# Input tiles whose high and low halves lie behind each other, at a fixed distance from the weight tiles

## The chip, the cores and the metric

The kernel runs on one core of a Trainium2 chip. The metric is the time of one execution in device microseconds; lower is better.

## The reference, cut to what matters

One inference step of a decoder trunk, for 256 prompt tokens and 8 x 4 sample tokens, 288 rows in all, in float32 with a model width of 2048:

```python
x = x + 0.5 * swiglu(rms_norm(x, norm_ffn1), ffn1_w_gu, ffn1_w_down)     # 2048 -> 2 x 5632 -> 2048
z = rms_norm(x, norm_mix) @ w_in                                         # 2048 -> 13600
o_ret, o_rwkv = retention(z, state_ret), rwkv7(z, state_rwkv, state_shift)
merged = sigmoid(zgr) * (o_ret @ w_ret_o) + sigmoid(zgw) * (o_rwkv @ w_rwkv_o)
x = x + merged @ w_out
x = x + 0.5 * swiglu(rms_norm(x, norm_ffn2), ffn2_w_gu, ffn2_w_down)
y = rms_norm(x, norm_final)                                              # and the new states
```

## The kernel before, in words

Everything is kept transposed: the model width lies on the 128 partitions, in tiles of `[128, T]` with T = 288 columns, one per token. An input of a matrix product is a row of such tiles, k = 0 to 15 (21 for g, 7 for ow), each 288 x 4 = 1152 bytes in each partition.

The large products are made more exact by splitting. Each float32 operand is written as a high part, rounded to TensorE's faster float32 form (F32R), and a low part, the rest. Weights arrive from HBM by the SP queue in blocks of `[128, 2048]`, 16 tiles of 128 x 128, into the two slots of `raw`. ACT copies a block into `w_hi` (line 1068, halves at a time in line 1077), DVE subtracts into `w_lo` (line 1495, or 1489), and a wait on `lo_made` lets TensorE start on the block; `used` gives the slots back. A down projection's block has 1408 columns. Inputs are split in the same way: `h_hi`, `h_lo` (normalized x, for the gate and up projections and most of the mixing projections), `g_hi`, `g_lo` (the hidden layer, lines 1133 and 1563, two tiles at a time), `xg_hi`, `xg_lo` (the normalized x of the first mixing projections), `or`, `ow` (the outputs of retention and RWKV) and `m` (merged, lines 1454 and 2130).

For each weight tile `products` in the tensor block issues three matmuls, and each brings its own weight load:

```python
pe.matmul(out, wh, xh, start=start, stop=False)      # line 528
pe.matmul(out, wh, xl, start=False, stop=False)      # line 529
return pe.matmul(out, wl, xh, start=False, stop=stop)  # line 530
```

`pair` (lines 533 to 557) walks over two output tiles and all k: for k, for m in 0 and 1, `products` with column tile 2k + m of the weights and input tile k, into PSUM bank m of the pair. `piece` (from line 631) does a sixteenth of a block in the same way; in the mixing stage `weave` sets such pieces between the steps of retention and RWKV, by the shares in GAPS, so that TensorE has work while DVE, ACT and GpSimd go through the serial steps. TensorE's order is that of the program; weight loads are shown as an engine of their own, PEld, and run beside the matmul before.

SBUF is laid out by hand. `sb` gives out addresses from a running place in steps of 32 bytes, or puts a tile at a given address. `raw` and `w_hi` take 16384 bytes each. Before the change `w_lo`, `h_hi` and `h_lo` follow directly, and all lie at the same place modulo 256; `g_hi`, `g_lo`, `m_hi`, `m_lo`, `ow_hi` and `ow_lo` start 64 bytes behind it modulo 256, `xg_hi` and `xg_lo` 192 bytes, `or_hi` 32 and `or_lo` 64 bytes. The high halves of all k stand together, and then the low halves of all k.

Of the kernel before, what the change touches and what calls it, by code (L numbers as in the profile page):

```python
# [23 lines left out]
F32, F32R = mybir.dt.float32, mybir.dt.float32r  # L24
ALU, ACT = mybir.AluOpType, mybir.ActivationFunctionType

P = 128
D = 2048
KT = D // P
FF = 5632  # L30
HALF = FF // 2
HT = HALF // P
SEQ, SB, ST = 256, 8, 4
NS = SB * ST
T = SEQ + NS
# [3 lines left out]
PAIRS = RW // P  # L39
# [21 lines left out]
GATE_PAIRS = 2 * D // (2 * P)  # L61
GATE_BLOCKS = 2 * GATE_PAIRS
PARTS = 16
LOW_AT = (3, 10)
FIRST_MIX = (2, 5, 8, 11, 14)

# [35 lines left out]
def parts(blocks):  # L102

    total, seen, out = sum(w for _, w in GAPS), 0, {}
    for name, w in GAPS:
        first = round(PARTS * blocks * seen / total)
        seen += w
        out[name] = range(first, round(PARTS * blocks * seen / total))
    return out
# [7 lines left out]
def build(nc, d):  # L117
    with ExitStack() as ctx:
        place = [-(-nc.sbuf_base // 32) * 32]

        def sb(name, shape, dt=F32, at=None):

            size = int(np.prod(shape[1:])) * 4
            offset = place[0] if at is None else at
            if at is None:
                place[0] += -(-size // 32) * 32
            return nc.alloc_sbuf_tensor_at("sb_" + name, list(shape), dt, offset=offset)
# [5 lines left out]


        raw = sb("raw", [P, 2, BLK])
        w_hi = sb("w_hi", [P, 2, BLK], F32R)
        w_lo = sb("w_lo", [P, 2, BLK], F32R)
        h_hi = sb("h_hi", [P, KT, T], F32R)
        h_lo = sb("h_lo", [P, KT, T], F32R)
        mean_w = sb("mean_w", [P, P])  # L140
        head_w = sb("head_w", [P, P], F32R)
        ident = sb("ident", [P, P])
        gains = sb("gains", [P, 4, KT])
        eps_c = sb("eps_c", [P, 2])
        first_root = sb("first_root", [P, 1])
        arena = place[0]


        x = sb("x", [P, KT, T])
        g_hi = sb("g_hi", [P, HT, T], F32R)  # L150
        g_lo = sb("g_lo", [P, HT, T], F32R)
        gate = sb("gate", [P, 2, T])
        prod = sb("prod", [P, 2, T])
        sq = sb("sq", [P, 2, T])
        sum_sq = sb("sum_sq", [P, 2, T])
        scale = sb("scale", [P, T])
        xg_at = place[0]
        xg_hi = sb("xg_hi", [P, KT, T], F32R)
        xg_lo = sb("xg_lo", [P, KT, T], F32R)
        first_sq = sb("first_sq", [P, KT, T], at=xg_at)  # L160
        ffn_end = place[0]

# [4 lines left out]
        mix = place[0]  # L167
# [14 lines left out]
        tri = sb("tri", [P, 2, CH])  # L182
        tri_s = sb("tri_s", [P, 2, CH])
        eye = sb("eye", [P, CH])
        own = sb("own", [P, SB])
        run_m = sb("run_m", [P, T])
        last = sb("last", [P, 6, 1 + SB])
        rot = sb("rot", [P, 2, T])
# [91 lines left out]
        gate_z = sb("gate_z", [P, 2, 2, T], at=zs_at)  # L280

        place[0] = mix
        or_hi = sb("or_hi", [P, RH * VT, T], F32R, at=qk_at)
        assert qk_at + 4 * RH * VT * T <= trig_end
        or_lo = sb("or_lo", [P, RH * VT, T], F32R, at=arena)
        part = sb("part", [P, KT, T], at=mix + 8 * KT * T)
        ow_at = mix + 12 * KT * T + 24 * T
        ow_hi = sb("ow_hi", [P, PAIRS, T], F32R, at=ow_at)
        ow_lo = sb("ow_lo", [P, PAIRS, T], F32R, at=ow_at + 4 * PAIRS * T)
        m_hi = sb("m_hi", [P, KT, T], F32R, at=mix)  # L290
        m_lo = sb("m_lo", [P, KT, T], F32R, at=mix + 4 * KT * T)
        gate_m = sb("gate_m", [P, 2, 2, T], at=mix + 12 * KT * T)
        prod_m = sb("prod_m", [P, 2, T], at=mix + 12 * KT * T + 16 * T)
        assert max(ffn_end, pair_end, ow_at + 8 * PAIRS * T) <= nc.sbuf_usable_end


# [129 lines left out]
        class Weave:  # L426
# [6 lines left out]
            def __call__(self, gap):  # L433
                assert self.left.pop(0) == gap, gap
                for n in self.share[gap]:
                    self.piece(*divmod(n, PARTS))

# [88 lines left out]
        def _(pe):  # L526
# [91 lines left out]
            def projections(i):  # L618
                for n in range(MIX_BLOCKS):
                    for q in range(PARTS):  # L620
                        if n == 2 and q == 0:
# [1808 lines left out]
```

## Time and profile before

| | us |
|---|---|
| median of 3 runs | 2896.09 (2895.13 to 2897.52) |
| span of the profiled execution | 2893.1 |
| TensorE busy in it | 2869.7 |
| weight loads (PEld) | 2797.0 |
| DVE | 1564.2 |
| ACT | 1116.4 |
| GpSimd | 107.0 |

The times are those of whole executions. The profiled execution is one of its own; its total is told by its span alone, from its first instruction to its last, and lies 3.0 us under the median of the runs. The span goes through the first feed-forward (to about 845 us), the mixing stage (to 1780 us, with the gates' projections at its end), the output projections (to 2035 us) and the second feed-forward. A group's line gives line, engine, operation, tiles written and read, shapes and count, then the busy time, the mean length of one record in ns, and the idle time before it. Records of matmuls overlap, and their ends are modelled: a start is measured, a length is not.

### The profile page before, as it was taken

Reading aid. Unit: us, or ns where it says so; the run is one execution under the profiler, and the core shown is the slowest. Engines: PE = TensorE matmul, PEld = TensorE weight load, DVE = VectorE, ACT = ScalarE, POOL = GpSimd, SP = SyncE. Lnnn points to the kernel's source line nnn. Section 1 sums busy time; section 2 is a strip of 40 time slices with the busy share of each in tenths; the row PEclk is TensorE's granted clock in tenths of the full one; section 3 lists DMA queues with packets and bytes.
Section 4 is the critical chain, followed back from the end, with each engine's and each line's share of the span. In section 5 each row is a group of like instructions: output and inputs, shape, how many; then the busy total and the mean of one; then the engine's idle time right before and its main releaser. Section 6 shows DMA issues by size and latency. Waiting matters only on the chain.

```text
span 2893.1 us, 57249 instructions
## 1 busy us (share of the span) xinstructions
PE 2869.7 (99%) x24662; PEld 2797.0 (97%) x24662; DVE 1564.2 (54%) x1679; ACT 1116.4 (39%) x1121; POOL 107.0 (4%) x144
## 2 busy tenths in 40 slices
PE   9999999999999999999999999999999999999998
PEld 9999999999999999898999999999999999999998
DVE  6444444444557576775765555465544444444454
ACT  5333333333344353544534644233333333333333
POOL 0000000000000002011020010000000000000000
PEclk9999999999999999999999999999999999999999
DMA  5444444444456553635436544555444444444444
GB/s 208 161 162 163 160 169 175 159 164 153 169 185 221 184 193 110 247 133 199 160 130 237 180 153 164 186 201 190 163 162 162 163 160 169 175 160 165 153 168 142
DMA packets 85460, 495.80 MB, mean 171 GB/s; under 512 B 10320, under 2 KB 10496, under 8 KB 44096
## 3 DMA queue, kind: packets, MB, share of 16 engines
q1 hardware_dynamic: 71424, 444.14, 43.5%
q0 software_dynamic: 9280, 32.72, 3.1%
q10 hardware_dynamic: 4608, 16.78, 1.5%
q8 instruction: 116, 1.90, 0.3%
q14 instruction: 32, 0.26, 0.0%
HBM read 462.80 MB, written 30.80 MB: 171 GB/s over the span
## 4 chain that ended last, share of the span: by engine, by line
PE 94%; DVE 3%; ACT 2%; DMA 1%; issue 0%; SPq 0%; ACTq 0%; DVEq 0%
PE psum L528 29%; PE psum L529 29%; PE psum L530 29%; PE psum L876 1%; DVE sb_w_lo L1489 1%; PE psum L692 1%; PE psum L728 0%; DMA sb_raw<-in_gu 0%; DMA sb_raw<-in_w_wo 0%; PE psum L649 0%; ACT sb_w_hi L1077 0%; DVE sb_w_lo L1495 0%; ACT sb_w_hi L1068 0%; PE psum L889 0%; PE psum L886 0%
## 5 line engine op out<-in xcount | busy, mean ns | idle before, releaser
L528 PE MATMUL psum<-sb_h_hi,sb_w_hi 128*128 128x288 f32 x4384 | 1315.3, 300 | 3.6 <-DVE sb_w_lo L1489 1.4
L530 PE MATMUL psum<-sb_h_hi,sb_w_lo 128*128 128x288 f32 x4384 | 1295.1, 295 | 0.0
L529 PE MATMUL psum<-sb_h_lo,sb_w_hi 128*128 128x288 f32 x4384 | 1294.0, 295 | 0.0
L1495 DVE TENSOR_TENSOR sb_w_lo<-sb_raw,sb_w_hi 128x2048 fp32r<-128x2048 f32 (+1 forms) x348 | 712.4, 2047 | 723.8 <-ACT sb_w_hi L1068 723.2
L1068 ACT ACTIVATE sb_w_hi<-sb_raw 128x2048 fp32r<-128x2048 f32 (+1 forms) x349 | 600.3, 1720 | 1226.9 <-PE psum L530 1191.9
L528 PEld LDWEIGHTS psum<-sb_h_hi,sb_w_hi 128*128 128x128 f32 x4384 | 824.6, 188 | 27.8 <-issue 18.9
L529 PEld LDWEIGHTS psum<-sb_h_lo,sb_w_hi 128*128 128x128 f32 x4384 | 824.6, 188 | 1.3 <-issue 1.0
L530 PEld LDWEIGHTS psum<-sb_h_hi,sb_w_lo 128*128 128x128 f32 x4384 | 824.9, 188 | 0.0
L529 PE MATMUL psum<-sb_g_lo,sb_w_hi 128*128 128x288 f32 x1408 | 416.8, 296 | 0.0
L530 PE MATMUL psum<-sb_g_hi,sb_w_lo 128*128 128x288 f32 x1408 | 414.9, 295 | 0.0
L528 PE MATMUL psum<-sb_g_hi,sb_w_hi 128*128 128x288 f32 x1408 | 413.8, 294 | 0.0
L1489 DVE TENSOR_TENSOR sb_w_lo<-sb_raw,sb_w_hi 128x1024 fp32r<-128x1024 f32 x204 | 254.0, 1264 | 119.9 <-ACT sb_w_hi L1077 116.0
L528 PEld LDWEIGHTS psum<-sb_g_hi,sb_w_hi 128*128 128x128 f32 x1408 | 264.8, 188 | 0.0
L530 PEld LDWEIGHTS psum<-sb_g_hi,sb_w_lo 128*128 128x128 f32 x1408 | 264.6, 188 | 0.0
L529 PEld LDWEIGHTS psum<-sb_g_lo,sb_w_hi 128*128 128x128 f32 x1408 | 264.6, 188 | 0.0
L1077 ACT ACTIVATE sb_w_hi<-sb_raw 128x1024 fp32r<-128x1024 f32 x198 | 198.7, 1053 | 140.1 <-PE psum L530 109.1
L1545 DVE TENSOR_TENSOR sb_prod<-psum,sb_scale 128x576 f32<-128x576 f32 x44 | 33.3, 757 | 93.8 <-PE psum L530 93.8
L1556 DVE TENSOR_TENSOR sb_gate<-psum,sb_scale 128x576 f32<-128x576 f32 x44 | 33.3, 757 | 84.1 <-PE psum L530 84.0
L528 PE MATMUL psum<-sb_or_hi,sb_w_hi 128*128 128x288 f32 x256 | 76.0, 297 | 0.0
L529 PE MATMUL psum<-sb_m_lo,sb_w_hi 128*128 128x288 f32 x256 | 75.8, 296 | 0.0
L530 PE MATMUL psum<-sb_m_hi,sb_w_lo 128*128 128x288 f32 x256 | 75.5, 295 | 0.0
L530 PE MATMUL psum<-sb_or_hi,sb_w_lo 128*128 128x288 f32 x256 | 75.4, 295 | 0.0
(380 smaller groups left out, 2391.4 us busy)
## 6 DMA issues: line engine op xcount, KB each, us to landing
sb_raw<-in_gu SPq DMA_DIRECT2D x175, 1024.0 KB, 4.8
sb_raw<-in_down SPq DMA_DIRECT2D x128, 704.0 KB, 4.0
sb_raw<-in_w_mix SPq DMA_DIRECT2D x72, 1024.0 KB, 4.9
sb_raw<-in_w_gates SPq DMA_DIRECT2D x32, 1024.0 KB, 5.4
sb_s_ret<-in_s_ret POOLq DMA_DIRECT2D x32, 512.0 KB, 8.1
out_ret_s<-sb_s_ret ACTq DMA_DIRECT2D x32, 512.0 KB, 5.3
sb_raw<-in_w_ro SPq DMA_DIRECT2D x16, 1024.0 KB, 4.8
sb_raw<-in_w_out SPq DMA_DIRECT2D x16, 1024.0 KB, 4.8
```

What stands on the lines that cost most here:

```text
L528: pe.matmul(out, wh, xh, start=start, stop=False)
L529: pe.matmul(out, wh, xl, start=False, stop=False)
L530: return pe.matmul(out, wl, xh, start=False, stop=stop)
L692: mm = pe.matmul(psum[j * NS:(j + 1) * NS, bank, :], q_own[:, e, SLOTS * half + j, :], s_ret[:, 2 * e + j // 2, j % 2, :], start=(e == 0 a ...
L876: mm = pe.matmul(psum[w, 5, (t - 1) * CH:t * CH], lm[v, t, :], xm[v, t, :], start=True, stop=True)
L1068: act.activation(w_hi[:, slot, 0:cols], raw[:, slot, 0:cols], ACT.Copy).then_inc(hi_made, 2)
L1077: act.activation(w_hi[:, slot, c], raw[:, slot, c], ACT.Copy).then_inc(hi_made, 1)
L1489: dve.tensor_tensor(w_lo[:, slot, c], raw[:, slot, c], w_hi[:, slot, c].bitcast(F32), ALU.subtract).then_inc(lo_made, 1)
L1495: dve.tensor_tensor(w_lo[:, slot, 0:cols], raw[:, slot, 0:cols], w_hi[:, slot, 0:cols].bitcast(F32), ALU.subtract).then_inc(lo_made, 2)
L1545: dve.tensor_tensor(prod[:, :, :], psum[:, s:s + 2, 0:T], twice(scale), ALU.mult).then_inc(up_scaled, 1)
L1556: dve.tensor_tensor(gate[:, :, :], psum[:, s:s + 2, 0:T], twice(scale), ALU.mult).then_inc(gate_scaled, 1)
```

## The change

It adds two constants and two helpers to the layout. `align(apart)` moves the running place on to a fixed distance behind `w_hi` modulo 256. `halves_of` makes one tile in which the high half of tile k is followed at once by its low half: a pair takes 2304 bytes, nine times 256. It starts 144 bytes behind `w_hi` modulo 256 (128 by `align`, and 16 by four elements that stay unused in front). `w_lo` is moved to 128 bytes behind `w_hi` modulo 256. h, g, xg, ow and m are made by `halves_of`; `or_hi` and `or_lo` stay as they are, apart from the shift of what lies before them. `own`, `eps_c` and `first_root` are moved into the space that aligning leaves. No instruction is added or taken away, and no wait, count or loop is changed; what the instructions read and write is the same data at other addresses.

```diff
@@ -61,6 +61,7 @@
 GATE_PAIRS = 2 * D // (2 * P)
 GATE_BLOCKS = 2 * GATE_PAIRS
 PARTS = 16
+LINES, APART = 256, 144
 LOW_AT = (3, 10)
 FIRST_MIX = (2, 5, 8, 11, 14)
 
@@ -133,30 +134,45 @@
 
 
         raw = sb("raw", [P, 2, BLK])
+        weights_at = place[0]
         w_hi = sb("w_hi", [P, 2, BLK], F32R)
+        eps_c = sb("eps_c", [P, 3])
+        first_root = eps_c[:, 2:3]
+        own = sb("own", [P, SB])
+
+        def align(apart):
+
+            place[0] += (weights_at + apart // 32 * 32 - place[0]) % LINES
+
+        def halves_of(name, tiles, at=None):
+
+            if at is None:
+                align(APART)
+            ahead = APART % 32 // 4
+            both = sb(name, [P, ahead + 2 * tiles * T], F32R, at=at)
+            both = both[:, ahead:].rearrange("p (k two t) -> p k two t", two=2, t=T)
+            return both[:, :, 0, :], both[:, :, 1, :]
+
+        align(4 * T % LINES)
         w_lo = sb("w_lo", [P, 2, BLK], F32R)
-        h_hi = sb("h_hi", [P, KT, T], F32R)
-        h_lo = sb("h_lo", [P, KT, T], F32R)
+        h_hi, h_lo = halves_of("h", KT)
         mean_w = sb("mean_w", [P, P])
         head_w = sb("head_w", [P, P], F32R)
         ident = sb("ident", [P, P])
         gains = sb("gains", [P, 4, KT])
-        eps_c = sb("eps_c", [P, 2])
-        first_root = sb("first_root", [P, 1])
         arena = place[0]
 
 
         x = sb("x", [P, KT, T])
-        g_hi = sb("g_hi", [P, HT, T], F32R)
-        g_lo = sb("g_lo", [P, HT, T], F32R)
+        g_hi, g_lo = halves_of("g", HT)
         gate = sb("gate", [P, 2, T])
         prod = sb("prod", [P, 2, T])
         sq = sb("sq", [P, 2, T])
         sum_sq = sb("sum_sq", [P, 2, T])
         scale = sb("scale", [P, T])
+        align(APART)
         xg_at = place[0]
-        xg_hi = sb("xg_hi", [P, KT, T], F32R)
-        xg_lo = sb("xg_lo", [P, KT, T], F32R)
+        xg_hi, xg_lo = halves_of("xg", KT)
         first_sq = sb("first_sq", [P, KT, T], at=xg_at)
         ffn_end = place[0]
 
@@ -182,7 +198,6 @@
         tri = sb("tri", [P, 2, CH])
         tri_s = sb("tri_s", [P, 2, CH])
         eye = sb("eye", [P, CH])
-        own = sb("own", [P, SB])
         run_m = sb("run_m", [P, T])
         last = sb("last", [P, 6, 1 + SB])
         rot = sb("rot", [P, 2, T])
@@ -280,17 +295,19 @@
         gate_z = sb("gate_z", [P, 2, 2, T], at=zs_at)
 
         place[0] = mix
+        align(APART)
+        m_at = place[0]
         or_hi = sb("or_hi", [P, RH * VT, T], F32R, at=qk_at)
         assert qk_at + 4 * RH * VT * T <= trig_end
         or_lo = sb("or_lo", [P, RH * VT, T], F32R, at=arena)
-        part = sb("part", [P, KT, T], at=mix + 8 * KT * T)
-        ow_at = mix + 12 * KT * T + 24 * T
-        ow_hi = sb("ow_hi", [P, PAIRS, T], F32R, at=ow_at)
-        ow_lo = sb("ow_lo", [P, PAIRS, T], F32R, at=ow_at + 4 * PAIRS * T)
-        m_hi = sb("m_hi", [P, KT, T], F32R, at=mix)
-        m_lo = sb("m_lo", [P, KT, T], F32R, at=mix + 4 * KT * T)
-        gate_m = sb("gate_m", [P, 2, 2, T], at=mix + 12 * KT * T)
-        prod_m = sb("prod_m", [P, 2, T], at=mix + 12 * KT * T + 16 * T)
+        part = sb("part", [P, KT, T], at=m_at + 8 * KT * T)
+        place[0] = m_at + 12 * KT * T + 24 * T
+        align(APART)
+        ow_at = place[0]
+        ow_hi, ow_lo = halves_of("ow", PAIRS, ow_at)
+        m_hi, m_lo = halves_of("m", KT, m_at)
+        gate_m = sb("gate_m", [P, 2, 2, T], at=m_at + 12 * KT * T)
+        prod_m = sb("prod_m", [P, 2, T], at=m_at + 12 * KT * T + 16 * T)
         assert max(ffn_end, pair_end, ow_at + 8 * PAIRS * T) <= nc.sbuf_usable_end
```

## Rows read from the trace of the kernel before

**Rows 1.** The page: span, busy time of each engine, chain that ended last.
```profile
span 2893.1 us, 57249 instructions
...
PE 2869.7 (99%) x24662; PEld 2797.0 (97%) x24662; DVE 1564.2 (54%) x1679; ACT 1116.4 (39%) x1121; POOL 107.0 (4%) x144
...
PE 94%; DVE 3%; ACT 2%; DMA 1%; issue 0%; SPq 0%; ACTq 0%; DVEq 0%
```

**Rows 2.** Groups of PE matmuls, shapes apart: line 528 by input; then 450 to 650 us.
```profile
L528 PE MATMUL psum<-sb_h_hi,sb_w_hi 128*128 128x288 f32 x4384 | 1315.3, 300 | 3.6 <-DVE sb_w_lo L1489 1.4 <-issue 1.3 <-DVE sb_w_lo L1495 0.4
...
L528 PE MATMUL psum<-sb_g_hi,sb_w_hi 128*128 128x288 f32 x1408 | 413.8, 294 | 0.0
L528 PE MATMUL psum<-sb_or_hi,sb_w_hi 128*128 128x288 f32 x256 | 76.0, 297 | 0.0
...
L528 PE MATMUL psum<-sb_m_hi,sb_w_hi 128*128 128x288 f32 x256 | 75.1, 293 | 0.0
...
L528 PE MATMUL psum<-sb_xg_hi,sb_w_hi 128*128 128x288 f32 x128 | 38.3, 299 | 0.4 <-DVE sb_w_lo L1489 0.2
...
L528 PE MATMUL psum<-sb_ow_hi,sb_w_hi 128*128 128x288 f32 x128 | 37.9, 296 | 0.8 <-DVE sb_w_lo L1495 0.8
...
L529 PE MATMUL psum<-sb_h_lo,sb_w_hi 128*128 128x288 f32 x503 | 148.6, 295 | 0.0
L530 PE MATMUL psum<-sb_h_hi,sb_w_lo 128*128 128x288 f32 x503 | 148.6, 295 | 0.0
L528 PE MATMUL psum<-sb_h_hi,sb_w_hi 128*128 128x288 f32 x502 | 147.8, 294 | 0.0
```

**Rows 3.** Windows: the mixing stage, then stretches with g, h, or, m.
```profile
core 0: us, PE busy (x) PEld busy (x) DVE busy (x) ACT busy (x) POOL busy (x), PEclk, DMA share, GB/s
850.00:1780.00 930.00, 924.13 (x10058) 856.82 (x10057) 601.28 (x960) 425.34 (x588) 101.27 (x130) 0.99 0.50 177
320.00:430.00 110.00, 110.00 (x834) 110.00 (x833) 45.18 (x31) 35.46 (x26) 0.00 (x0) 1.00 0.50 170
450.00:650.00 200.00, 200.00 (x1508) 200.00 (x1508) 94.54 (x63) 68.26 (x46) 0.00 (x0) 1.00 0.46 163
1788.00:1868.00 80.00, 80.00 (x607) 80.00 (x606) 37.98 (x28) 26.91 (x21) 0.00 (x0) 1.00 0.55 199
1940.00:2030.00 90.00, 90.00 (x683) 90.00 (x682) 53.88 (x49) 32.78 (x28) 3.22 (x6) 1.00 0.52 185
```

**Rows 4.** Waits of all engines, then PE's: total us, times, longest us.
```profile
ACT sb_w_hi L1068 <- PE psum L530: 1191.9, 325, 5.0
...
PE psum L573 <- DVE sb_prod L1513: 1.8, 1, 1.8
PE psum L528 <- DVE sb_w_lo L1489: 1.7, 5, 0.4
```

**Rows 5.** Timeline of PE: start us, length us, instruction; fp32 matmuls.
```profile
1033.99 1.08 PE L748 MATMUL psum<-sb_rc,sb_o_s 128*128 128x32 f32 x8 [0.45 <-DVE sb_s_ret L1866]
...
857.81 0.89 PE L563 MATMUL psum<-sb_sum_sq,sb_mean_w 128*128 128x288 f32 x3
858.53 0.41 PE L567 MATMUL psum<-sb_sq,sb_mean_w 128*128 128x288 f32 x1
```

**Rows 6.** Single records (mean ns of one), then the timeline of PE from 2458 us.
```profile
L528 PE MATMUL psum<-sb_m_hi,sb_w_hi 128*128 128x288 f32 x1 | 0.3, 289 | 0.0
...
L528 PE MATMUL psum<-sb_h_hi,sb_w_hi 128*128 128x288 f32 x1 | 0.3, 302 | 0.0
...
2458.44 0.37 PE L528 MATMUL psum<-sb_h_hi,sb_w_hi 128*128 128x288 f32 x1 [0.21 <-DVE sb_w_lo L1495]
...
2460.11 0.29 PE L528 MATMUL psum<-sb_h_hi,sb_w_hi 128*128 128x288 f32 x1
...
2460.89 0.30 PE L528 MATMUL psum<-sb_h_hi,sb_w_hi 128*128 128x288 f32 x1
...
2461.70 0.29 PE L528 MATMUL psum<-sb_h_hi,sb_w_hi 128*128 128x288 f32 x1
```

**Rows 7.** Groups of DVE and ACT, shapes apart.
```profile
L1495 DVE TENSOR_TENSOR sb_w_lo<-sb_raw,sb_w_hi 128x2048 fp32r<-128x2048 f32 x220 | 504.4, 2293 | 468.5 <-ACT sb_w_hi L1068 467.9 <-DVE sb_gate L1556 0.4 <-DVE sb_sum_sq L1533 0.2
L1068 ACT ACTIVATE sb_w_hi<-sb_raw 128x2048 fp32r<-128x2048 f32 x221 | 423.5, 1916 | 866.1 <-PE psum L530 836.4 <-DMA sb_raw<-in_w_wo 25.1 <-DMA sb_raw<-in_w_out 4.5
...
L1545 DVE TENSOR_TENSOR sb_prod<-psum,sb_scale 128x576 f32<-128x576 f32 x44 | 33.3, 757 | 93.8 <-PE psum L530 93.8
```

## Prediction, made before any run of the change

> **What bounds the kernel now.** I read the page's busy line first: TensorE is busy for 2869.7 of 2893.1 us, and the chain that ended last runs through it for 94% [rows 1]. Only some 23 us of the span are without a matmul, so the change can matter only by making the matmuls themselves cheaper or dearer. The groups say which: the three products of each weight tile, lines 528 to 530. The tiles of one of them are 4384 with h, 1408 with g, 256 with or, 256 with m, 128 with xg and 128 with ow [rows 2], together 6560, or 19680 products. A record of these matmuls is 294.7 ns long in a stretch of products alone (294, 295 and 295 [rows 2]), but records overlap and their ends are modelled; what costs time is the spacing of their starts. In a stretch of products alone the windows give it [rows 3]: 1508 records in 200 us, less the 2.2 that only hang over the edges (0.295 us by 0.133 us), is 132.8 ns with h; 834 in 110 us is 132.3 ns with g; 607 in 80 us is 132.3 ns with or; 683 in 90 us is 132.2 ns with m. So 19680 products at about 132.6 ns are 2610 us, nine tenths of the span. The granted clock there is 1.00, which is 2.4 GHz, and 288 columns at one per clock are 120 ns. Some 12.5 ns of each product go to something else.
>
> What is it? Three readings. It is not waiting: of PE's waits the longest sum is 1.8 us in the whole span [rows 4]. It is not the weight load alone: eight products that stream only 32 columns behind a load of 128x128 take 1.08 us in all, and less one record of 0.28 us that is 0.80 us for seven spacings, 115 ns each [rows 5]. Nor is it a fixed price of every matmul: the fp32 product of line 563, which streams its 288 columns at half rate beside the same load, is spaced (0.89 - 0.41)/2 = 0.24 us, which is 288 columns at 1.2 per ns and nothing more [rows 5]. The 12 ns appear where a full-rate stream runs beside a load. That is what two reads of one memory that get in each other's way would look like, and the length of single records points to the addresses: one of line 528 with m is 289 ns long, one of the same line with h 302 ns [rows 6], though instruction, shape and neighbours are the same. Their lengths are modelled, so I assume that a record's length and its spacing go together, 294.7 ns with 132.7.
>
> **The addresses.** Before, w_hi, w_lo and h start at 0 modulo 256, a weight tile is 512 bytes and an input tile 1152, that is 128 modulo 256. While a product streams, the next product's tile is loaded. So the distance from that load alternates with k: 0 and 128 with h, 64 and 192 with g, m, ow and xg, and with or 32 and 160 (high) or 64 and 192 (low). After, an input tile pair is 2304 bytes, 0 modulo 256, and low lies 128 behind high; w_lo is moved by 128 too. High against w_hi is 144; low while w_lo loads is 16 - 128 = 144; high while the next w_hi loads is 144. Every product outside or (768 of them) then has one distance, always the same: 19680 - 768 = 18912 products.
>
> **Part by part.** No instruction, wait or DMA is added, removed or reordered on any queue; only addresses move, and first_root joins eps_c. (1) The 18912 products: price unknown, bounded by the nearest rows. Lower end: every record as the shortest one, 289 ns; against 294.7 that is 5.7 ns, 108 us less. Beyond that lies only the bare stream, 12.5 ns or 236 us less, which no full-rate row comes near. Upper end: every record as the longest one, 302 ns, 7.3 ns or 138 us more. I take the lower end, 5.7 ns: a stream whose every product has the same relation should repeat one spacing instead of cycling through short and long ones, and of the two ends 289 ns is the nearer to the means of whole groups, 293 with m and 294 with g [rows 2]. This is a choice; the rows hold no distance with an odd number of 16-byte steps, and 144 is one. (2) The writers: the pairs that ACT and DVE write into g, m are now two runs instead of one. DVE already reads two runs of 288 in two PSUM banks at 757 ns for 576 elements [rows 7], some 1.3 ns each, hardly more than the 1.1 ns of the one long run in line 1495 (2293 ns for 2048) [rows 7]; and both engines stand idle half the time [rows 1]. Cost nothing. (3) The weights' own preparation: 1916 ns on ACT and 2293 ns on DVE [rows 7] for a block that feeds 48 products, 6.37 us now and 6.10 us after. ACT waits 1191.9 us in 325 times for PE, 3.7 us per block [rows 4]; 0.27 us less leaves it ample. The DMA share is 0.46 to 0.55 [rows 3]; 4% more is ample too. If this cover were gone, PE would wait for line 1495. (4) The mixing stage, 850 to 1780 us: PE stands still for only 6 us there now, because pieces of projections fill the steps of retention and RWKV [rows 3]. Of its 1696 tiles (4384 with h less the 2 x 22 x 64 = 2816 of the two feed-forwards, and 128 with xg), 5088 products, 28 us would be saved; the serial steps on DVE, ACT and POOL stay as long, so some waits come out behind shorter pieces. I give back a fifth, 5 us; ends 0 and 15. (5) The 768 products with or and the small matmuls: nothing, ends -3 and +3.
> Sum: -108 + 5 = -103 us. The profiled execution spans 2893.1 us, 3.0 us under the median of 2896.09; I carry that 3 us over unchanged: 2790.1 + 3.0 = 2793 us.
>
> **A rule that speaks against it.** The rows show a full-rate stream beside a load 12 ns over 120 [rows 3, 5]. The Trainium skill (TensorE: Matmul & The Clock Gate, Step-by-step: what each phase is for) says that the engine has two independent read ports, and that loading the next weights doesn't steal read bandwidth from the running matmul. By it no address could matter, and the time would stay at 2896: rival (a).
>
> **The rivals.** (a) **Nothing moves.** The loss is a property of the pair load and stream, not of where they lie. For: the four stretches lie at four mixtures of distances, and all are spaced 132.2 to 132.8 ns [rows 3]; a mere reshuffle of stalls inside a cycle would look like that. Against: the record lengths. At most h takes m's spacing: 4384 x 3 x 0.5 ns = 7 us, so 2889 to 2899 us. (b) **144 lies on the wrong side.** Its nearest rows are the products at 128. Counting six products for each k from the first with h at 2458.44, k = 2 (distance 0) lasts from 2460.11 to 2460.89, 0.78 us, and k = 3 (distance 128) until 2461.70, 0.81 us [rows 6]. The mean lies between the two, so products that were all like those of k = 3 would be dearer by half the gap: 0.015 us over six, 2.5 ns each. As each start is rounded to 10 ns, I take 1 ns as likely and 2.5 as the limit; over 18912 products that is +19 us, 2915 us, and at the limit 2943. It decides from the point where the mean record of line 529 is over 295 ns. No other engine is involved. (c) **Half of it.** The steady relation removes only the long records: spacing 130 to 131 ns, 2 ns less, -38 us, 2858 us.
>
> **How the numbers follow.** Forecast (spacing 126 to 129 ns, 2765 to 2840): 0.45. Rival (c): 0.17. Rival (a): 0.15, of which a sliver is faster by more than 0.2%. Rival (b): 0.23. A measurement of this kernel tells about 0.2%, 6 us, from no change. Faster 0.62, same 0.15, slower 0.23. The range has to reach from the forecast's low end to rival (b)'s likely value: 2760 to 2917; below lie some 0.05 (nearer the bare stream), above 0.1. As both signs have a share, the forecast's own range of 2765 to 2840 stands beside it. I hold the forecast likelier than (b), whose rows are nearer, because 0.03 us of difference in one cycle can be the cost of changing over between two distances, which the new layout no longer does.
>
> **What would show it.** Right: in 450 to 650 us some 1577 records (200 us by 0.127, and 2.2) instead of 1508 [rows 3], records with h, g and m of one length near 289 ns, those with or unchanged at 293 to 297, PE busy still 99%, and g faster by as much as h. The order of short and long records gone, three products repeating. Wrong: counts of 1505 to 1512 (rival a), or under 1500 with records of 296 ns and more (rival b). If PE's waits for DVE grow past 30 us, the mixing stage is where point (4) was too small.

## The result and the profile after

The changed kernel takes 2867.72 us (median of 4 runs, 2866.13 to 2868.89) against 2896.04 for the kernel before (4 runs on the same chip, 2895.13 to 2897.52): a ratio of 0.9899, 95% interval 0.9885 to 0.9913. It is 28.3 us faster. 2793 was predicted, 103 us less; the sign was right, but less than a third of the size came.

The page of the kernel after: span, busy time, chain that ended last. These answer to [rows 1].

```profile
span 2867.0 us, 57289 instructions
...
PE 2841.1 (99%) x24662; PEld 2768.5 (97%) x24662; DVE 1564.2 (55%) x1679; ACT 1117.0 (39%) x1121; POOL 107.2 (4%) x144
...
PE 93%; DVE 3%; ACT 2%; DMA 1%; issue 0%; SPq 0%; ACTq 0%; DVEq 0%; POOLq 0%
```

As many matmuls as before are busy for 28.6 us less, and the span is 26.1 us shorter. DVE, ACT and POOL work as long as before. (The 40 more instructions are register operations of DVE's sequencer, which count as no busy time.) So the gain lies in the time of the matmuls. The windows, which answer to [rows 3]:

```profile
core 0: us, PE busy (x) PEld busy (x) DVE busy (x) ACT busy (x) POOL busy (x), PEclk, DMA share, GB/s
320.00:430.00 110.00, 109.75 (x838) 109.55 (x836) 46.53 (x32) 36.03 (x26) 0.00 (x0) 1.00 0.50 170
450.00:650.00 200.00, 200.00 (x1528) 200.00 (x1526) 96.89 (x64) 69.50 (x49) 0.00 (x0) 1.00 0.47 165
850.00:1780.00 930.00, 922.96 (x10121) 856.27 (x10120) 606.08 (x964) 427.50 (x590) 96.49 (x121) 1.00 0.50 179
1788.00:1868.00 80.00, 80.00 (x604) 80.00 (x604) 32.81 (x19) 24.71 (x13) 0.00 (x0) 1.00 0.50 180
1940.00:2020.00 80.00, 80.00 (x612) 80.00 (x611) 48.88 (x44) 30.07 (x27) 2.69 (x5) 1.00 0.50 180
```

With h there are 1528 records in 200 us: less the 2.2 at the edges 131.1 ns a product, where it was 132.8. With m 612 in 80 us are 131.2 ns; with or 604 are 132.9 ns, a little more than before. The window with g also reaches over the end of that stage, where the first product of the next starts 0.55 us after the last one; taken from the starts themselves, the spacing of g is 131.11 ns as well (it was 132.22), and that of h 131.11 (it was 132.78). With h and g three products take 393.33 ns throughout, which is 472 clocks of 1.2 GHz.

What the three look like is in the groups of 450 to 650 us (as in [rows 2]), and in the timeline of PE from 500 us (start us, length us, instruction):

```profile
L547 PE MATMUL psum<-sb_h,sb_w_lo 128*128 128x288 f32 x509 | 150.7, 296 | 0.0
L546 PE MATMUL psum<-sb_h,sb_w_hi 128*128 128x288 f32 x510 | 150.4, 295 | 0.0
L545 PE MATMUL psum<-sb_h,sb_w_hi 128*128 128x288 f32 x509 | 147.1, 289 | 0.0
```
```profile
500.01 0.29 PE L545 MATMUL psum<-sb_h,sb_w_hi 128*128 128x288 f32 x1
...
500.40 0.29 PE L545 MATMUL psum<-sb_h,sb_w_hi 128*128 128x288 f32 x1
500.53 0.29 PE L546 MATMUL psum<-sb_h,sb_w_hi 128*128 128x288 f32 x1
500.66 0.30 PE L547 MATMUL psum<-sb_h,sb_w_lo 128*128 128x288 f32 x1
500.80 0.29 PE L545 MATMUL psum<-sb_h,sb_w_hi 128*128 128x288 f32 x1
...
501.19 0.29 PE L545 MATMUL psum<-sb_h,sb_w_hi 128*128 128x288 f32 x1
```

Line 545 is the old 528. Its record is 289 ns now, every time, and the next product starts 126.7 ns after it (mean of the starts; the timeline rounds to 10 ns). Line 546 has 295 ns and 131.7, line 547 296 ns and 135.0. The three products have one distance and still three lengths, and their mean is what the kernel pays: 131.1 ns. From 500.01 to 501.19 three rounds pass, 1.18 us.

The waits of PE (total us, times, longest us) stay as small as in [rows 4]:

```profile
PE psum L545 <- DVE sb_w_lo L1506: 2.1, 5, 0.4
PE psum L545 <- issue: 1.9, 2, 1.7
PE psum L590 <- DVE sb_prod L1530: 1.8, 1, 1.8
```

By the spacings 28.4 us were to be expected: 13152 products with h by 1.67 ns are 22.0 us, 4224 with g by 1.11 are 4.7, 1536 with m, xg and ow by 1.1 are 1.7; and 0.4 go back with or (768 by 0.55). Both kernels issue the same matmuls in the same order, so each stage can be timed from one matmul to the same matmul in the other trace. The feed-forwards give 9.6 and 9.3 us (9.4 each by the products), the output projections 0.2, the start costs 0.3, and the mixing stage gives 7.2 where its products promise 8.3. Together that is the 26.1 us of the spans.

But 2.9 of those 7.2 us have nothing to do with addresses. The granted clock fell from 1.00 to 0.50, that is from 2.4 to 1.2 GHz, for some 7 us at a time, twice in the mixing stage before (near 1313 and 1491 us) and once after. The stretch of the second fall, before and after, 90 matmuls each:

```profile
1489.00:1499.00 10.00, 10.00 (x96) 8.53 (x95) 2.25 (x8) 4.16 (x6) 0.00 (x0) 0.66 0.32 107
```
```profile
1477.00:1485.00 8.00, 8.00 (x112) 6.94 (x108) 3.16 (x9) 4.16 (x6) 0.40 (x1) 1.00 0.36 133
```

The same 90 matmuls take 10.1 us before and 7.2 after. So the addresses are worth 4.3 us in the mixing stage, half of what its products promise, and 23.2 us of the 26.1 in this pair of traces. The number of such falls also moves the times of one kernel: beside the next experiments the kernel before took 2888.32 us at a mean granted clock of 0.998 and 2901.39 at 0.994. Those 13 us are 0.4%; the ratio's interval starts 0.9% from 1.

### The profile page after: what moved, and what is told of

It reads as the page before. It is cut to its first block, busy times and chain, and to the rows that moved or that the text cites. A ratio compares the mean times of both kernels' runs of the same rounds, so it can differ in the third digit from the quotient of the medians.

```text
span 2867.0 us, 57289 instructions
## 1 busy us (share of the span) xinstructions
PE 2841.1 (99%) x24662; PEld 2768.5 (97%) x24662; DVE 1564.2 (55%) x1679; ACT 1117.0 (39%) x1121; POOL 107.2 (4%) x144
## 4 chain that ended last, share of the span: by engine, by line
PE 93%; DVE 3%; ACT 2%; DMA 1%; issue 0%; SPq 0%; ACTq 0%; DVEq 0%; POOLq 0%
PE psum L545 29%; PE psum L546 29%; PE psum L547 29%; PE psum L893 1%; PE psum L709 1%; DVE sb_w_lo L1506 1%; DMA sb_raw<-in_w_wo 0%; DMA sb_raw<-in_gu 0%; PE psum L666 0%; ACT sb_w_hi L1094 0%; DVE sb_w_lo L1512 0%; ACT sb_w_hi L1085 0%; PE psum L906 0%; PE psum L903 0%; PE psum L745 0%
## 5 line engine op out<-in xcount | busy, mean ns | idle before, releaser
L547 PE MATMUL psum<-sb_h,sb_w_lo 128*128 128x288 f32 x4384 | 1297.7, 296 | 0.0
L546 PE MATMUL psum<-sb_h,sb_w_hi 128*128 128x288 f32 x4384 | 1293.9, 295 | 0.0
L545 PE MATMUL psum<-sb_h,sb_w_hi 128*128 128x288 f32 x4384 | 1288.5, 294 | 4.2 <-DVE sb_w_lo L1506 1.7
L545 PEld LDWEIGHTS psum<-sb_h,sb_w_hi 128*128 128x128 f32 x4384 | 828.4, 189 | 28.5 <-issue 19.9
L547 PEld LDWEIGHTS psum<-sb_h,sb_w_lo 128*128 128x128 f32 x4384 | 823.9, 188 | 0.0
L546 PEld LDWEIGHTS psum<-sb_h,sb_w_hi 128*128 128x128 f32 x4384 | 821.5, 187 | 1.3 <-issue 1.0
L547 PE MATMUL psum<-sb_g,sb_w_lo 128*128 128x288 f32 x1408 | 416.8, 296 | 0.0
L546 PE MATMUL psum<-sb_g,sb_w_hi 128*128 128x288 f32 x1408 | 415.4, 295 | 0.0
L545 PE MATMUL psum<-sb_g,sb_w_hi 128*128 128x288 f32 x1408 | 407.0, 289 | 0.0
L545 PEld LDWEIGHTS psum<-sb_g,sb_w_hi 128*128 128x128 f32 x1408 | 266.1, 189 | 0.0
L547 PEld LDWEIGHTS psum<-sb_g,sb_w_lo 128*128 128x128 f32 x1408 | 264.3, 188 | 0.0
L546 PEld LDWEIGHTS psum<-sb_g,sb_w_hi 128*128 128x128 f32 x1408 | 263.3, 187 | 0.0
L546 PE MATMUL psum<-sb_or_lo,sb_w_hi 128*128 128x288 f32 x256 | 75.9, 297 | 0.0
L547 PE MATMUL psum<-sb_m,sb_w_lo 128*128 128x288 f32 x256 | 75.8, 296 | 0.0
```

## The experiments

The distance between two addresses is meant modulo 256 throughout: of the moving operand behind the weight tile that is loaded while it streams.

**Distances by themselves.** Behind the usual start, groups of 36 products with the same weight tile and the same moving operand, one group for each distance; a short matmul stands between the groups. The kernel follows unchanged.

```diff
+            for c in BENCH_D:
+                many([(w[0], bench_x(c), P, T)])
...
+                for rows in (64, 32):
+                    many([(w[2], bench_x(c), rows, T)])
```

> The changed kernel with some 2000 extra matmuls ahead of the first product (their results are not used), in groups of 36 that repeat one matmul, one moving tile and one weight tile, 288 columns, with the moving tile 0, 16, ... 240 bytes behind the weight tile modulo 256, and a few groups at odd distances, shorter loads, shorter and longer streams, and plain float32. Theory 1, the distance between stream and load sets the spacing, and 144 is one good value: the 16 groups differ by 2 ns and more, those at 144 are spaced 131.1 ns (what 1528 records in 200 us give) and among the shortest, those at 0 and 128 133 to 135 ns. Theory 2, only that the distance never changes matters: all 16 groups are spaced 131.1 ns within 0.3. Theory 3, the loss is a fixed price of stream beside load: all 16 groups at one value, and loads of 64 or 32 columns don't lower it. If stalls come from overlap with the load, loads of 64 columns cost about half the 11 ns over 120, loads of 32 a quarter, and a stream of 512 columns loses the same 11 ns as one of 288 while the float32 one loses 0 to 2.

The timeline of PE, groups at 0, 48, 128 and 144 bytes:

```profile
13.96 5.00 PE L607 MATMUL psum<-sb_bench 128*128 128x288 f32 x36
...
29.36 4.95 PE L607 MATMUL psum<-sb_bench 128*128 128x288 f32 x36
...
54.91 5.06 PE L607 MATMUL psum<-sb_bench 128*128 128x288 f32 x36
...
60.07 4.95 PE L607 MATMUL psum<-sb_bench 128*128 128x288 f32 x36
```

Over the last 24 starts of each group, the spacing is 131.67 ns at 0, 133.33 at 128 and 130.00 at 144 and 48, the lowest of the sixteen. So an address can move it by 3.3 ns, nothing else being changed, and the 127 ns that the forecast needed are nowhere. The sixteen were taken again in falling order with another weight tile: 144 gave 130.00 again, 48 this time 132.5. Places off the 16-byte steps were worse, up to 136.0 ns at 136 bytes. A distance of 400 (144 and one 256 more) gave 131.1, one of 656 gave 130.0. Smaller loads hardly help: with 64 columns 130.0 ns at 0 and 129.4 at 144, with 32 columns 131.1 and 130.0. Plain fp32 products, each of which shows as two records, have their records 242.5 ns apart.

**One relation, but another one.** APART = 128 puts every product at 128, by the same three moves as at 144.

```diff
-LINES, APART = 256, 144
+LINES, APART = 256, 128
```

> The changed kernel with the distance 128 instead of 144 bytes, so that every product still has one unchanging distance, but an even number of 16-byte steps. Theory 1, the distance itself matters, and 128 is a worse one (its products lasted longer before): spacing 132.8 ns or more and 2896 us or more, up to 2943. Theory 2, an unchanging distance is all that is needed: 131.1 ns and 2868 us as with 144.

It takes 2907.37 us (10 runs, 2900.42 to 2908.66), ratio 1.0040 with 1.0027 to 1.0052: slower than before. Its windows:

```profile
320.00:430.00 110.00, 110.00 (x827) 110.00 (x827) 45.19 (x31) 34.61 (x25) 0.00 (x0) 1.00 0.50 167
450.00:650.00 200.00, 200.00 (x1502) 200.00 (x1502) 95.07 (x63) 69.27 (x48) 0.00 (x0) 1.00 0.46 164
```

1502 records are 133.3 ns with h, 827 in 110 us 133.4 with g. Interleaving the halves and giving all products the same distance bring nothing by themselves; with the distance 144 they do.

**The kernel's own walk, at every distance.** Groups of 96 products that read as `products` does, k by k, in the layout before (stride 1152) and after (stride 2304, low half 1152 behind, w_lo at 128), at 0 to 240; then single tiles with one operand broadcast from one element.

```diff
+            for c in (0, 64, 192):
+                like(c, 4 * T, 8 * 4 * T, 0)
+            for c in range(0, 256, 16):
+                like(c, 8 * T, 4 * T, 128)
+            like(144, 8 * T, 4 * T, 0)
...
+            for c in (0, 144):
+                flat = tile(bx + c, 1).broadcast_to([P, T])
+                many([(tile(0), flat, 6)])
+                many([(tile(0, 1).broadcast_to([P, P]), tile(bx + c, T), 6)])
...
+            for c in (128, 144):
+                for n in range(16, 256, 32):
+                    many([(tile(n), tile(bx + n + c, T), 6)])
```

> The changed kernel with some 4600 extra matmuls ahead of the first product (their results are not used). Most are groups of 96 that walk through weights and inputs as the products do: 16 weight tiles of 512 bytes, two PSUM banks, high, low, high, with 8 input pairs 2304 bytes apart, at 16 distances; the same with pairs 2560 bytes apart, so that the distance is one modulo 512 and not only modulo 256; and the old layout at distances 0, 64 and 192. Theory 1, the distance sets the spacing: at 2304 bytes the group at 144 is spaced 131.1 ns, at 128 133.3 ns as in the kernel with 128, most others between 131 and 134, and the old layout 132.2 to 132.8. If the period is 512 (single-tile groups gave 130.0 ns at 144 and 656, 131.1 at 400) the group at 2560 bytes and 144 is spaced 130.0 ns; if it is 256, 131.1 ns. Theory 4, the stall comes from the stream's own reads or from the write into PSUM and not from the load's: a stream that reads one element over and over at the distances 0 and 144 gives whether SBUF reads matter (120 to 123 ns if the stream's reads stall, 130 and more if not), and loads that read one column over and over leave the spacing where it was (if the load's reads stalled it, they bring it to 120 to 123). Moving weight tile and stream together through SBUF, at 128 or 144 apart: by theory 1 the spacings stay 133.3 and 130.0; if the stream's own address counted, they change.

The layouts of before give 132.8 ns at 0 (h, as in the kernel), 132.2 at 192, and 132.8 at 64, where the kernel has 132.2 with g. The new one gives 131.1 at 144 and at 208 alone; 133.3 to 133.5 at 0, 32, 96, 112, 128, 160, 176, 224 and 240; 132.0 at 80, the rest between. With w_lo at 0 instead of 128, the 144 gives 133.3. A stride of 2560 bytes repeats these within 0.2 ns, apart from 0 itself (131.1). So the stride hardly counts; the relation does, and both halves of it. From 60 us on DVE, ACT and the DMA queues stand idle during these walks, so what they do in the kernel isn't needed for the effect.

The absolute place counts too. Two of the groups that move a single weight tile and its stream through SBUF together, 144 bytes apart, the weight tile at 16 and at 48 bytes:

```profile
663.48 6.61 PE L615 MATMUL psum<-sb_bench 128*128 128x288 f32 x48
...
670.20 6.61 PE L615 MATMUL psum<-sb_bench 128*128 128x288 f32 x48
```

All eight groups at 144, with the weight tile at 16, 48 ... 240 bytes, have 132.2 ns, where the tile at 0 had 130.0; by the relation alone they would have kept 130.0. (At 128 apart all eight keep 133.3.) The grid below varies the relation only, with the high weights at 0.

The one-element operands (moving and loaded, at 0, then two PSUM banks, then moving at 144):

```profile
569.91 6.28 PE L615 MATMUL psum<-sb_bench 128*128 128x288 f32 x48
...
576.30 6.60 PE L615 MATMUL psum<-sb_bench 128*128 128x288 f32 x48
...
583.01 6.59 PE L615 MATMUL psum<-sb_bench 128*128 128x288 f32 x48
...
589.70 6.28 PE L615 MATMUL psum<-sb_bench 128*128 128x288 f32 x48
```

A moving operand read from one element makes the spacing 125.3 ns, whatever the distance; a weight tile from one column leaves 132.0 at 0 (129.3 at 144). So some 5.3 ns of the 12 over the bare stream stay wherever the one element lies, and the rest, 5 to 8 ns at most places, goes when the stream no longer reads 288 different elements.

**The low weights back at 0.** The kernel after, with w_lo where it was modulo 256; the middle product of each three then has distance 16.

```diff
-        align(4 * T % LINES)
         w_lo = sb("w_lo", [P, 2, BLK], F32R)
+        eps_c = sb("eps_c", [P, 3])
+        first_root = eps_c[:, 2:3]
+        own = sb("own", [P, SB])
```

> The changed kernel with the low weights back at 0 modulo 256 (eps_c and own moved behind them). The low input's product then runs at 16 bytes from the load beside it, the two others stay at 144. Theory 1: as 16 alone gave 131.7 ns and 144 gave 130.0 to 131.1, the spacing goes up by 0.3 to 1 ns, 2874 to 2887 us. Theory 2, an unchanging distance is what counts: back to 132.2 to 132.8 ns, 2889 to 2900 us. Theory 3, the low weights' place does nothing: 2868 us.

2906.94 us (7 runs, 2900.32 to 2909.14), ratio 1.0038 (1.0023 to 1.0054). The window of 450 to 650 us holds 1502 records, 133.3 ns, as in the walk by itself:

```profile
450.00:650.00 200.00, 200.00 (x1502) 200.00 (x1501) 94.98 (x63) 69.29 (x48) 0.00 (x0) 1.00 0.46 164
```

The three spacings are 131.7, 134.8 and 133.4 ns, where the kernel after had 126.7, 131.7 and 135.0. Only the middle product has another distance, and the first two became dearer by 5.0 and 3.1 ns, the third cheaper by 1.6: no product has a price of its own, the round of three has one. None of the three expectations had 2907 us.

**The whole grid.** Walks of 48 products with the high input at a and the low weights at wl, 16 by 16 places.

```diff
+            for a in range(0, 256, 16):
+                for wl in range(0, 256, 16):
+                    like(a, 8 * T, 4 * T, wl, 1)
```

> The changed kernel with 256 groups of 48 extra matmuls ahead of the first product (results not used). Each group walks as the products do (pairs 2304 bytes apart, low 1152 behind high) for one pair of places: high input 0, 16 ... 240 bytes behind the high weights, low weights 0, 16 ... 240 bytes behind the high ones, modulo 256. Theory 1, each product's distance from the load beside it adds its part: the groups differ by up to 3 ns; at 144 and 128 the spacing is 131.1 ns and at 144 and 0 133.3 ns, as in the groups and kernels before; and a pair of places below 131.1 ns may exist, down to the 130.0 ns that single tiles gave at 144. Theory 5, the cycle locks only to whole steps of 8 clocks of 1.2 GHz over three products: then most groups lie at 131.1 (472 clocks for three), 133.3 (480), and none between 128.9 and 131.0.

Most of the 256 cells are at 131.1, 132.2 or 133.3 ns. (144, 128), the change's, is at 131.12, as some 65 others; the extremes are (144, 48) with 128.88 and (112, 0) with 130.00 below, 135.6 above. Nothing comes near 126. Theory 5, whole steps over three products, is too narrow: 132.2 ns comes out even over six products, and 130.00 is 58.5 steps over three.

**The two lowest cells in the kernel.** First LOW_APART = 48:

```diff
-LINES, APART = 256, 144
+LINES, APART, LOW_APART = 256, 144, 48
...
+        ahead = LOW_APART % 32 // 4
+        w_lo = sb("w_lo", [P, ahead + 2 * BLK], F32R)[:, ahead:].rearrange("p (s b) -> p s b", b=BLK)
```

> The changed kernel with the low weights 48 bytes behind the high ones modulo 256 instead of 128; the distances are then 144, 224 and 144 instead of three times 144. In the sweep this was the shortest of 256 groups, 128.9 ns against 131.1. If the sweep carries over (theory 1 in the form that the whole cycle of distances counts, not that all are 144): spacing 128.9 ns, 18912 x 2.2 = 42 us less than the changed kernel, 2826 us. If what matters is that all three distances are 144, as the change has it, or if the sweep's group only had not settled yet: 131.1 ns or more, 2868 to 2910 us.

> The changed kernel with the high input at 112 instead of 144 bytes and the low weights at 0: distances 112, 240, 112. The sweep gave 130.0 ns. If it carries over, 18912 x 1.1 = 21 us less than the changed kernel, 2847 us, though its distances are neither equal nor 144; if an equal distance is needed, 132 to 133.3 ns, 2885 to 2910 us.

The first takes 2844.31 us (5 runs, 2833.88 to 2860.42), ratio 0.9818 with 0.9792 to 0.9845: faster than both kernels. The second (APART = 112, w_lo at 0) takes 2872.97 (3 runs, 2864.74 to 2881.94), ratio 0.9910 with 0.9889 to 0.9931: no faster than the change. A fourth run took 2908.88 us and is not in that ratio; its granted clock was that of the others, and it has no profile. The two scatter by 27 and 17 us, where four runs of the change lie within 3. The granted clock doesn't explain it: of the first kernel's runs, 2837.43 and 2853.70 us both had 0.998. The profiles, of the slowest run of the first kernel and of a run of the second, say why; h in the second and in the last feed-forward stages, first of w_lo at 48, then of 112:

```profile
450.00:650.00 200.00, 200.00 (x1554) 200.00 (x1553) 98.96 (x66) 70.94 (x49) 0.00 (x0) 1.00 0.47 168
2450.00:2650.00 200.00, 200.00 (x1477) 200.00 (x1476) 92.70 (x61) 67.30 (x46) 0.00 (x0) 1.00 0.45 160
```
```profile
450.00:650.00 200.00, 200.00 (x1541) 200.00 (x1540) 96.92 (x64) 70.90 (x48) 0.00 (x0) 1.00 0.47 168
2100.00:2260.00 160.00, 160.00 (x1182) 160.00 (x1182) 74.15 (x51) 54.38 (x37) 0.00 (x0) 1.00 0.45 162
```

Same instructions, same addresses, same clock: 1554 records in one stage, 1477 in another, 128.9 and 135.6 ns (130.0 and 135.6 in the other kernel). A stage falls into one round or another and keeps it, here for some 400 us from 2417 us to the end.

**Does the entry decide?** 69 layouts, each walked six times, behind one matmul of 64 to 264 columns.

```diff
+                for e in range(6):
+                    mark()
+                    pe.matmul(psum[:, 5, 0:64 + 40 * e], tile(0), tile(bx, 64 + 40 * e), start=True, stop=True)
+                    like(a, 8 * T, 4 * T, wl, 1)
```

> The changed kernel with extra matmuls ahead of the first product (results not used): for 69 places that were spaced 131.1 ns or less in the sweep, and for the old layout, the same group six times, each time entered behind a matmul of another length; then single-tile groups: streams of 256 to 512 columns that read one element over and over, and the 16 distances behind loads of 32 columns instead of 128. Theory 6, a layout has a few cycles it can settle in, and how it is entered decides which: at 144 and 48 the six entries give 128.9 ns and sometimes 135.6, at 112 and 0 130.0 and 135.6, at 144 and 128 always 131.1 (every stage of the changed kernel had it), the old layout 132.2 and 132.8. If the layout alone decides, the six entries agree everywhere. For the load: if its reads take read slots from the stream, loads of 32 columns (a quarter of the reads) lose a quarter of the 10 to 13 ns and the distances hardly differ; if only the start or the phase between the two counts, they still lose 10 to 13 ns, and still by the distance. The one-element streams are spaced 5 ns over the bare stream at every length if that part is a price per matmul.

(144, 128) is 131.1 from all six. (144, 48) is 128.9 four times and 135.5 twice; (112, 0) 130.0 twice and 135.6 four times; others have 131.1 and 133.3. The layouts of before give 132.2 or 132.8. The change's layout is one of those that showed a single round, which fits runs that agree. (0, 128) shows one too, 131.1 ns six times and in the grid, yet the longer walk of 96 products gave it 133.3; so six entries don't find every round.

The loads of 32 columns, at 0, 16 and 96 bytes:

```profile
43.47 4.91 PE L625 MATMUL psum<-sb_bench 128*32 128x288 f32 x36
...
48.49 4.96 PE L625 MATMUL psum<-sb_bench 128*32 128x288 f32 x36
...
73.58 4.84 PE L625 MATMUL psum<-sb_bench 128*32 128x288 f32 x36
```

Their spacings are 131.1, 133.3 and 128.9 ns, and those of all sixteen places lie between 128.9 and 133.3, on average 130.5 against 132.2 behind loads of 128 columns. A quarter of the load's reads leaves 10.5 of 12.2 ns, and still by the distance. So the loss isn't in proportion to what the load reads. A one-element stream of 256, 384 and 512 columns was timed in the same run: 112.0, 165.3 and 218.6 ns, each 5.3 over its columns at 2.4 per ns, as with 288.

**Can the program choose the entry?** The kernel with w_lo at 48 once with two short matmuls ahead of each stage of up and down projections, and once more as it was.

```diff
+                        if enter and u == 0:
+                            pe.matmul(psum[0:32, 7, 0:32], w_hi[:, slot, 0:32].bitcast(F32), hi[:, k, 0:32].bitcast(F32), start=True, stop=True)
+                            pe.matmul(psum[:, 7, 0:64], w_hi[:, slot, 0:P], hi[:, k, 0:64], start=True, stop=True)
```

> Layout of low48 (low halves of the weights 48 bytes behind the high ones), with two small products whose results nobody reads ahead of each feed-forward stage, so that the long row of products is entered from another state of TensorE. Theory (the layout has two repeating cycles, 128.9 and 135.6 ns a product, and what stands just before a stage decides which one it falls into; in the measurement of walks by themselves the entry behind short products gave 128.9): all eight up and down stages at 128.9 to 129.0 ns, so 2825 to 2832 us in every run. Rival (the cycle is decided by something that the program does not set, such as the moment at which the first weights land): some stages still at 135.6 ns, different ones from run to run, times spread from 2834 to 2860 us as in low48.

> The kernel low48 once more, unchanged. If the cycle of each stage is decided by what the program issues before it, the profile shows the same stages at 135.6 ns as before (the last two feed-forward stages, from 2416 us on) and the times lie near each other; if it is decided by moments that differ from run to run, other stages are the slow ones and the times spread over 2834 to 2860 us again.

With the two matmuls it takes 2847.78 us (5 runs, 2834.15 to 2850.13), ratio 0.9814 (0.9793 to 0.9835); unchanged 2846.92 (6 runs, 2836.05 to 2861.44), 0.9837 (0.9810 to 0.9864). Their intervals overlap, so no difference is shown. The repeat's own profile, again h in the two stages, its span 2834.2 us:

```profile
450.00:650.00 200.00, 200.00 (x1554) 200.00 (x1553) 98.95 (x66) 71.00 (x49) 0.00 (x0) 1.00 0.47 168
2450.00:2650.00 200.00, 200.00 (x1554) 200.00 (x1554) 98.11 (x65) 72.19 (x50) 0.00 (x0) 1.00 0.48 171
```

The last stages, slow in the first profile, are at 128.9 ns in this one; their 3168 products by 6.7 ns are 21 of the 24.4 us between the two spans (2858.6 and 2834.2 us). The same program enters the same stage in either way from run to run. The version with two matmuls had the first half of the first feed-forward at 131.1 ns (838 records in 320 to 430 us against 851), a third round of the same layout that none of its six entries had shown, and the products with m at 135.6:

```profile
320.00:430.00 110.00, 109.75 (x838) 109.50 (x837) 46.55 (x32) 36.04 (x26) 0.00 (x0) 1.00 0.51 170
```

So these two matmuls don't settle the round, and something that differs between runs has a say. What is issued just before has one too, by the six entries, but no way to hold the fast round was found. What sets it, the moment at which the first weights land for instance, was not tried.

## Why the prediction was right or wrong

**What bounds the kernel: right.** TensorE's products did it, and their spacing moved with nothing but addresses. Of the signs named, PE stayed busy for 99% and three products repeat; 1528 records lie between the 1505 to 1512 of rival (a) and the 1577 of the forecast, the lengths stayed unequal, and g gained less than h (1.11 ns against 1.67).

**Point (1), the 18912 products: this is the step that failed.** That addresses move the spacing was right; the size, and the reason given for it, were not. 5.7 ns each was taken, 1.5 was measured (1.2 in the two traces, without the stretch of the low clock). The premise that a record's length goes with its spacing holds within the round: the record of 289 ns is followed by 126.7 ns, those of 295 and 296 by 131.7 and 135.0. What failed is "a stream whose every product has the same relation should repeat one spacing". It repeats a round of three unequal ones, and at 128, with a relation just as steady, it is slower than before. The 289 ns of [rows 6] was one place in such a round, not a length that all products can have; the mean of all three lines went from 294.7 to 293.3 ns, a drop of 1.4, about what the spacing gave. [Rows 2] had the sign of it: not one group of all products with one input was below 293. The bare stream that the prediction named beyond its lower end seems out of reach too: 5.3 ns of the 12.5 stay with a moving operand of one element, at either distance. That leaves some 7 ns for addresses, an estimate. The fp32 products of [rows 5], from which the prediction took that there is no fixed price, show 2.5 ns by themselves (242.5 less 240): one spacing read from stamps rounded to 10 ns could not tell. Of the 256 places in the grid the lowest gave 3.9 ns less than the 132.8 of h before.

**The addresses: in the main right as to what counts, wrong as to why 144.** The relation counts, though the absolute place does too. The same distance for all is neither needed nor enough: 128 for all is worse than before by 0.4%, some 12 us, and (144, 48), with a middle product at another distance, is the best. The prediction noted that no row holds a distance with an odd number of 16-byte steps; that was the place where it had no evidence. That the sign came out right is luck: 144 is one of two distances out of sixteen, in the walk of 96 with w_lo at 128, that gain more than 1 ns on h, and it gains only with w_lo at such a place.

**Point (2), the writers: right.** DVE is busy for 1564.2 us as before, ACT for 1117.0 against 1116.4. **Point (3), the preparation: right** at this pace, where PE waits 2.1 us for line 1506 in all, and also at 128.9 ns, with 2.8 us in the repeat of w_lo at 48. **Point (4), the mixing stage: the part that comes back was taken too small.** A fifth was given back of what its products save; 4.0 of 8.3 us came back, nearly half, once the stretch of the low clock is set aside. The 5 us meant for a gain of 28 us (5088 by 5.7 ns is 29) are near 4.0 only because the gain itself was so much smaller. Only 1.2 us of it show as more idle time of PE (7.0 us against 5.9); where the rest goes stays open. **Point (5): +0.4 us with or,** within its ends; these products were to stay as they were, and their spacing rose from 132.2 to 132.8 ns.

**The rule against it.** The kernels at 144 and at 128 issue the same instructions and differ by 2.2 ns a product. That loading the next weights doesn't steal read bandwidth, as the Trainium skill has it (TensorE: Matmul & The Clock Gate, Step-by-step: what each phase is for), is therefore not the whole account of a pair of load and stream. But at distance 0 a load from one column saved nothing (132.0 against 131.7), one of 32 columns 0.6 ns, and a stream from one element 6.3 ns; so a loss of bandwidth in proportion to the load's reads is no account either. The same page of the Trainium skill (Wait — 56ns, not 53.3ns?) gives a fixed 2.5 ns for each matmul at 2.4 GHz; the fp32 records agree (242.5 ns for 240), the F32R ones with a one-element stream have 5.3.

**The rivals.** (a) is out by the ratio's interval. (b) is out for 144, but what it says of 128 came true: its estimate of 1 ns a product (2915 us) came near that kernel's 2907. Its price for each product by its own distance did not hold, as w_lo at 0 shows. (c), spacing 130 to 131 ns, was the nearest at 2858 us, 10 off. It would have been the better forecast: it asked for a smaller step away from the group means, and those were what the rows showed.

**What stays open.** Why the places of load and stream set the round's length, why the absolute place matters beside the relation, why nearly every round looked at, of one to fifteen products, is a whole number of steps of 8 clocks of 1.2 GHz (472 for three at 131.1 ns, 464 at 128.9, 488 at 135.6), and what chooses between the rounds of one layout. Whether the halves need to be interleaved at all wasn't tried: no kernel kept the old order and moved the tiles.

## What to carry to other kernels

Where TensorE is the bound and each product brings its own load, the places of weights and moving operand modulo 256 bytes are worth a per cent or two (here medians of 2844 to 2907 us for one program), so measure before laying out. Walks measured by themselves foretold the kernel's spacing to 0.2 ns where a layout showed one round. Where it has more they give a list that needn't be complete. Take a mean over a whole round, never its shortest record, as what a layout may reach. A layout with one round seems steady; one with a faster and a slower round (here 128.9 and 135.6 ns) may win on average and still scatter by 1%.

## What was not expected of the hardware

One program at the same addresses and the same clock runs whole stages at 128.9 or 135.6 ns a product, and keeps what it fell into. A stream that reads one element again and again is 5 to 6 ns quicker than one that reads 288.

In the first of the runs with single tiles 36 products of 128 columns took longer than 36 of 256 or 384, which looks like a price of short streams and is one of the clock. The groups, and windows inside the first two:

```profile
244.98 7.94 PE L607 MATMUL psum<-sb_bench 128*128 128x128 f32 x36
...
259.38 4.57 PE L607 MATMUL psum<-sb_bench 128*128 128x256 f32 x36
...
264.06 6.54 PE L607 MATMUL psum<-sb_bench 128*128 128x384 f32 x36
```
```profile
245.00:252.00 7.00, 7.00 (x34) 7.00 (x34) 0.00 (x0) 0.00 (x0) 0.00 (x0) 0.50 0.01 2
259.60:263.80 4.20, 4.20 (x36) 4.15 (x35) 0.00 (x0) 0.00 (x0) 0.00 (x0) 1.00 0.00 0
```

That is 213 ns apart for 128 columns at a granted clock of 0.50, and 120 for 256 at 1.00. Before, 36 products of 64 columns behind loads of 128x128 were 112 ns apart until the clock fell among them, and 213 from there on; the 192 columns that came after had 213 and then some 112, when the clock was back. So short streams behind such a load are spaced 112 ns whether they have 64 or 192 columns, and nearly twice that at half the clock. A benchmark of short matmuls has to be read with the granted clock beside it.
